# Expert weights of a mixture-of-experts stage loaded as two 1 MB transfers for each 2 MB slot

## The reference

```python
logits = (xt @ w_router + b_router).astype(jnp.float32)
top_vals, top_idx = lax.top_k(logits, TOP_K)          # 4 of 32 experts for each token
gates = jax.nn.softmax(top_vals, axis=-1)
...
def expert_block(args):
    xb, e = args
    hgu = xb @ w_up_gate[e] + b_up_gate[e]            # [1024, 2048]: 8 MB
    x_glu = jnp.minimum(hgu[:, :D_EXPERT], SWIGLU_LIMIT)
    x_lin = jnp.clip(hgu[:, D_EXPERT:], -SWIGLU_LIMIT, SWIGLU_LIMIT)
    hact = x_glu * jax.nn.sigmoid(SWIGLU_ALPHA * x_glu) * (x_lin + 1.0)
    return hact @ w_down[e] + b_down[e]               # [1024, 1024]: 4 MB
```

## Time and profile before

| | |
|---|---|
| Time, median of 3 runs | 1893.27 us (1886.38, 1893.27, 1894.21) |
| The profiled execution | 1885.67 us, its span 1883.9 us, mean granted TensorE clock 0.988 |
| TensorE matmuls busy | 1760.2 us, 93% of the span |
| VectorE, ScalarE, GpSimd busy | 774.7, 499.6, 209.3 us |
| DMA | 554.26 MB, 294 GB/s over the span, queue q1 72.6% |

### The profile page before, as it was taken

One profiled execution on the slowest core, in us unless ns is written; L12 is line 12 of the kernel. 1 busy time (PEld: TensorE's weight loads), 2 busy tenths in 40 slices (PEclk: granted clock), 3 DMA queues, 4 the chain that ended last, 5 costly groups with the idle time before them and its releaser, 6 DMA issues. The chain is left out here.

```text
span 1883.9 us, 28671 instructions
## 1 busy us (share of the span) xinstructions
PE 1760.2 (93%) x11617; PEld 1096.0 (58%) x11617; DVE 774.7 (41%) x1312; ACT 499.6 (27%) x784; POOL 209.3 (11%) x150
## 2 busy tenths in 40 slices
PE   8999999999999898988889889999999999999997
PEld 7774333333333333333333368978998768858996
DVE  7956111111111111111011186947555767346555
ACT  5644000000000000000000056436443331225552
POOL 5552000000000000000000045430000100410000
PEclk9999999999999999999999999999999989899999
DMA  7289999999999999999999946475530622256530
GB/s 285 101 310 403 383 426 428 430 430 429 430 429 430 431 429 430 429 430 430 430 429 429 398 142 260 159 266 204 197 134 21 209 92 53 105 179 225 193 118 34
DMA packets 104729, 554.26 MB, mean 294 GB/s; under 512 B 17442, under 2 KB 27683, under 8 KB 79219
## 3 DMA queue, kind: packets, MB, share of 16 engines
q1 hardware_dynamic: 104370, 553.25, 72.6%
q10 hardware_dynamic: 288, 0.02, 0.0%
HBM read 551.15 MB, written 2.10 MB: 294 GB/s over the span
## 5 line engine op out<-in xcount | busy, mean ns | idle before, releaser
L1365 PE MATMUL banks<-front,xsT 128*64 128x512 f32 x1344 | 298.4, 594 | 14.1 <-DMA front<-in_w_up 13.6
L1581 DVE TENSOR_SCALAR xT<-banks 128x512 f32<-128x512 f32 x32 | 22.1, 692 | 625.4 <-PE banks L1372 625.4
L1365 PEld LDWEIGHTS banks<-front,xsT 128*64 128x64 f32 x1344 | 95.7, 137 | 209.6 <-issue 178.4
L1405 PE MATMUL banks<-front,hT 128*64 128x512 f32 x704 | 159.3, 606 | 15.9 <-ACT hT L1480 15.9
L2356 PE MATMUL banks<-f_xT_hi,f_w_hi 128*128 128x256 f32 x512 | 144.9, 283 | 3.0 <-DVE f_xT_lo L319 3.0
L1476 ACT ACTIVATE xT<-xT 128x512 f32<-128x512 f32 x32 | 20.1, 629 | 475.4 <-DVE xT L1581 475.3
L2356 PE MATMUL banks<-f_xT_hi,f_w_lo 128*128 128x256 f32 x512 | 144.9, 283 | 0.0
L2356 PE MATMUL banks<-f_xT_lo,f_w_hi 128*128 128x256 f32 x512 | 144.9, 283 | 0.0
L1405 PEld LDWEIGHTS banks<-front,hT 128*64 128x64 f32 x704 | 50.2, 139 | 109.8 <-issue 99.3
L1710 POOL TENSOR_TENSOR p_w_lo<-p_w_raw,p_w_hi 128x1024 fp32r<-128x1024 f32 x4 | 11.6, 2929 | 910.0 <-ACT p_w_hi L1752 910.0
L2445 DVE TENSOR_TENSOR f_w_lo<-f_ring,f_w_hi 128x1024 fp32r<-128x1024 f32 x64 | 77.9, 1225 | 63.1 <-ACT f_w_hi L2398 63.1
(11 more groups left out here) (474 smaller groups left out, 3071.0 us busy)
## 6 DMA issues: line engine op xcount, KB each, us to landing
front<-in_w_up SPq DMA_DIRECT2D x84, 2048.0 KB, 32.9
front<-in_w_down SPq DMA_DIRECT2D x44, 2048.0 KB, 34.3
f_ring<-in_ffn_w SPq DMA_DIRECT2D x30, 2048.0 KB, 7.6
m_early_slots<-in_w_up SPq DMA_DIRECT2D x22, 2048.0 KB, 27.9
more_slots<-in_w_up SPq DMA_DIRECT2D x22, 2048.0 KB, 33.0
m_early_slots<-in_w_down SPq DMA_DIRECT2D x20, 2048.0 KB, 37.1
g_ring<-in_sgu_in SPq DMA_DIRECT2D x7, 2048.0 KB, 7.6
m_raw<-in_w_in SPq DMA_DIRECT2D x6, 2048.0 KB, 8.2
```

The source lines that it names most:

```text
L1365: ins = nc.tensor.matmul(c.banks[CAP * h:CAP * (h + 1), bank, :], xsT[:, k, :], up[:, o:o + BANK], start=k == 0, stop=False)
L1405: ins = nc.tensor.matmul(c.banks[CAP * h:CAP * (h + 1), DOWN, :], hT[:, at:at + CAP], down[:, o:o + BANK], start=k == 0, stop=k == KC - 1)
L1581: v.tensor_scalar(glu[:, :], c.banks[:, GLU, :], LIMIT, None, ALU.min).then_inc(glu_ready, 1)
```

## The change

Each load of a slot becomes two transfers, of columns 0 to 2047 and 2048 to 4095 of the slot, 1 MB each, and each half has a landing semaphore of its own. TensorE waits for a half before the first chunk that reads it (one chunk of up, two chunks of down) and counts `up_used` and `down_used` by halves, twice as many for an item. SyncE waits for the half of the old load that lies where the half of the new one goes. All thresholds are doubled to match. The order of the loads, the slots, the matmuls and the bytes are the same. The early loads of the mixer stage go in halves too, behind the same waits as before. `product` is that of itertools. The core of the diff:

```diff
+HALVES, HALF_SLOT = 2, SLOT // 2
-        self.up_in = [sem(f"up_in{q}") for q in range(UPS)]
+        self.up_in = [[sem(f"up_in{q}_{half}") for half in range(HALVES)] for q in range(UPS)]
...
-    def load_up(self, sp, e, q, slot=None, landed=None):
-        sp.dma_start(slot or self.slot(UP_SLOT[q]), self.dram["w_up"][bass.ds(e * P, P), q * SLOT:(q + 1) * SLOT]).then_inc(
-            landed or self.up_in[q], 16)
+    def load_up(self, sp, e, q, slot=None, landed=None, halves=range(HALVES)):
+        slot = slot if slot is not None else self.slot(UP_SLOT[q])
+        for half in halves:
+            at = half * HALF_SLOT
+            sp.dma_start(slot[:, at:at + HALF_SLOT],
+                         self.dram["w_up"][bass.ds(e * P, P), q * SLOT + at:q * SLOT + at + HALF_SLOT]).then_inc(
+                (landed or self.up_in[q])[half], 16)
...
                 def item(n, one):
-                    for s in range(FRONT):
+                    for s, half in product(range(FRONT), range(HALVES)):
...
-                                sp.wait_ge(up_used, n * (3 * UPS) + ((one + ago) * UPS + last + 1))
+                                sp.wait_ge(up_used, n * (3 * UPS * HALVES) + (
+                                    ((one + ago) * UPS + last) * HALVES + half + 1))
...
-                            load(n * 3 + one, s, lap_and_slot(flat)[1])
+                            load(n * 3 + one, s, lap_and_slot(flat)[1], (half,))
...
-                def weights(i, n):
+                def weights(i, n, half):
...
-                        pe.wait_ge(landed[at], i[0] * 32 + 16 * (lap + 1))
+                        pe.wait_ge(landed[at][half], i[0] * 32 + 16 * (lap + 1))
...
-                        if k % 2 == 0:
-                            up = weights(i, k // 2)
+                        up = weights(i, k // 2, k % 2)
...
-                        if k % 2 and k < KC - 1:
+                        if k < KC - 1:
                             ins.then_inc(up_used, 1)
...
-                        if j == 0:
-                            down = weights(i, UPS + half)
+                        if j % 2 == 0:
+                            down = weights(i, UPS + half, j // 2)
...
-                        if j == KC // 2 - 1:
+                        if j % 2:
                             ins.then_inc(down_used, 1)
...
-                    act.wait_ge(down_used, i * DOWNS + DOWNS)
+                    act.wait_ge(down_used, i * (DOWNS * HALVES) + DOWNS * HALVES)
...
-                    dve.wait_ge(up_used, i * UPS + UPS)
+                    dve.wait_ge(up_used, i * (UPS * HALVES) + UPS * HALVES)
```

More of the change, by code:

```diff
@@ L1 @@
 from contextlib import ExitStack
+from itertools import product
 import numpy as np
@@ L142, in open_experts @@
             "router_in", "r_const_in", "list_in", "b_down_in"))
-        self.up_in = [sem(f"up_in{q}") for q in range(UPS)]
-        self.down_in = [sem(f"down_in{h}") for h in range(DOWNS)]
-        self.early_in = [sem(f"early_in{q}") for q in range(EARLY)]
+        self.up_in = [[sem(f"up_in{q}_{half}") for half in range(HALVES)] for q in range(UPS)]
+        self.down_in = [[sem(f"down_in{h}_{half}") for half in range(HALVES)] for h in range(DOWNS)]
+        self.early_in = [[sem(f"early_in{q}_{half}") for half in range(HALVES)] for q in range(EARLY)]
     def slot(self, i):
@@ L151, in early_slot, with load_down @@
         return self.early_slots[:, i * SLOT:(i + 1) * SLOT]
-    def load_up(self, sp, e, q, slot=None, landed=None):
-        sp.dma_start(slot or self.slot(UP_SLOT[q]), self.dram["w_up"][bass.ds(e * P, P), q * SLOT:(q + 1) * SLOT]).then_inc(
-            landed or self.up_in[q], 16)
-    def load_down(self, sp, e, h, slot=None, landed=None):
-        sp.dma_start(slot or self.slot(DOWN_SLOT[h]), self.dram["w_down"][bass.ds(e * (2 * P) + h * P, P), :]).then_inc(
-            landed or self.down_in[h], 16)
+    def load_up(self, sp, e, q, slot=None, landed=None, halves=range(HALVES)):
[5 more added lines that the diff above has]
+                (landed or self.up_in[q])[half], 16)
+    def load_down(self, sp, e, h, slot=None, landed=None, halves=range(HALVES)):
+        slot = slot if slot is not None else self.slot(DOWN_SLOT[h])
+        for half in halves:
+            at = half * HALF_SLOT
+            sp.dma_start(slot[:, at:at + HALF_SLOT],
+                         self.dram["w_down"][bass.ds(e * (2 * P) + h * P, P), at:at + HALF_SLOT]).then_inc(
+                (landed or self.down_in[h])[half], 16)
     def load_expert_tables(self, sp):
@@ L1103, in expert_stage @@
         slots += [more[:, i * SLOT:(i + 1) * SLOT] for i in (1, 0)]
-        landed = c.up_in + c.down_in + c.early_in + [sem(f"slot_in{i}") for i in range(FRONT + EARLY, SPARE + 1)]
+        landed = c.up_in + c.down_in + c.early_in + [
+            [sem(f"slot_in{i}_{half}") for half in range(HALVES)] for i in range(FRONT + EARLY, SPARE + 1)]
         squares = slots[RING - 1][:, 0:TC * D].rearrange("p (c n) -> p c n", c=TC)
@@ L1191, in _, with load @@
             def _(sp):
-                def load(e, n, at):
+                def load(e, n, at, halves=range(HALVES)):
                     if n < UPS:
-                        c.load_up(sp, e, n, slots[at], landed[at])
+                        c.load_up(sp, e, n, slots[at], landed[at], halves)
                     else:
-                        c.load_down(sp, e, n - UPS, slots[at], landed[at])
+                        c.load_down(sp, e, n - UPS, slots[at], landed[at], halves)
                 def item(n, one):
-                    for s in range(FRONT):
+                    for s, half in product(range(FRONT), range(HALVES)):
                         flat = FRONT * one + s
@@ L1204, in item @@
                             if last < UPS:
-                                sp.wait_ge(up_used, n * (3 * UPS) + ((one + ago) * UPS + last + 1))
-                            else:
-                                sp.wait_ge(down_used, n * (3 * DOWNS) + ((one + ago) * DOWNS + last + 1 - UPS))
+                                sp.wait_ge(up_used, n * (3 * UPS * HALVES) + (
+                                    ((one + ago) * UPS + last) * HALVES + half + 1))
+                            else:
+                                sp.wait_ge(down_used, n * (3 * DOWNS * HALVES) + (
+                                    ((one + ago) * DOWNS + last - UPS) * HALVES + half + 1))
                         if flat == RING:
-                            load(one, s, SPARE)
-                            sp.wait_ge(root_done, 1)
-                            load(one, s - 1, RING - 1)
+                            load(one, s, SPARE, (half,))
+                            if half == HALVES - 1:
+                                sp.wait_ge(root_done, 1)
+                                load(one, s - 1, RING - 1)
                         elif flat >= FRONT + EARLY and flat != RING - 1:
-                            load(n * 3 + one, s, lap_and_slot(flat)[1])
+                            load(n * 3 + one, s, lap_and_slot(flat)[1], (half,))
                 def late_item(i, e):
-                    for s in range(FRONT):
+                    for s, half in product(range(FRONT), range(HALVES)):
                         if s < UPS:
-                            sp.wait_ge(up_used, i * UPS + (s + 1 - UPS))
+                            sp.wait_ge(up_used, i * (UPS * HALVES) + ((s - UPS) * HALVES + half + 1))
                         else:
-                            sp.wait_ge(down_used, i * DOWNS + (s - UPS + 1 - DOWNS))
-                        load(e, s, lap_and_slot(FRONT * (E - 1) + s)[1])
+                            sp.wait_ge(down_used, i * (DOWNS * HALVES) + ((s - UPS - DOWNS) * HALVES + half + 1))
+                        load(e, s, lap_and_slot(FRONT * (E - 1) + s)[1], (half,))
                 sp.dma_start(chooser[:, :], c.dram["chooser"]).then_inc(chooser_in, 16)
@@ L1233, in _ @@
                     late_item(i, listed_at(sp, i + EXPERT_AT, E - 1))
-                sp.wait_ge(down_used, DOWNS * (E - 1))
+                sp.wait_ge(down_used, DOWNS * HALVES * (E - 1))
                 c.next_embedding.load(sp)
@@ L1344, in weights @@
                     if isinstance(i, tuple):
-                        pe.wait_ge(landed[at], i[0] * 32 + 16 * (lap + 1))
+                        pe.wait_ge(landed[at][half], i[0] * 32 + 16 * (lap + 1))
                     elif isinstance(i, int):
-                        pe.wait_ge(landed[at], 16 * (lap + 1))
+                        pe.wait_ge(landed[at][half], 16 * (lap + 1))
                     else:
-                        pe.wait_ge(landed[at], i * 16 + 16 * (lap + 1 - (E - 1)))
+                        pe.wait_ge(landed[at][half], i * 16 + 16 * (lap + 1 - (E - 1)))
                     return slots[at]
```

## The result

| | Before | Changed |
|---|---|---|
| Median of 22 runs each | 1886.29 us (1878.84 to 1894.21) | 1894.54 us (1887.08 to 1902.51) |
| Ratio to before | | 1.0036, 95% interval 1.0020 to 1.0052 |
| The profiled execution, its span | 1885.67, 1883.9 us | 1900.08, 1898.3 us |

The changed kernel is slower by 0.36%, 6.8 us of 1886.29 (3.8 to 9.8); the two medians are 8.25 us apart, which lies in that interval. The interval is clear of 1, the size is within the 0.5% that the prediction called no change, and the forecast was 15.4 us. Two of the three runs that the prediction had for a base lay at the upper end of what 22 runs show, and so did their median, 1893.27. Of the 14.2 us between the forecast 1908.7 and the median measured, 7.0 are the base, and the other 7.2 are the size of the change.

The account below looks back on a forecast made before the run. DMA, busy without a gap through the expert stage, was taken as the bound. 19.0 us for shorter rows less 1.8 at the gap and 1.8 at the tail gave +15.4 on the median 1893.27: 1908.7 us, range 1894 to 1919.

Parts of the forecast that it names:

- The bound: Expert stage: DMA busy without a gap at 429.5 GB/s, 29.30 us an expert; TensorE needs 27.2 and late on follows DMA.
- The gap: DMA runs dry near 218 us, waiting for expert 1's first down slot; reloading by halves restarts it earlier, gain 1.8 us.
- The tail: Last expert: TensorE starts on the first half of the last up slot while the second lands, gain 1.8 us.
- The edits at nothing: TensorE's added waits, SyncE's added issues, doubled thresholds and the embedding weights behind the expert loads: claimed to cost nothing.
- The time of a slot: Expert loads: rows of 8 KB instead of 16 KB cost 0.110 us a slot, 19.0 us over 173 loads.
- the division of the rows into queued transfers and lone ones: Price of an added packet: 11.8 to 13.8 ns where transfers queue, 5.6 to 5.7 ns alone; expert loads counted as queued.
- the 435 GB/s rival: Expert stage: twice the transfers keep the queue fuller and DMA at 435 GB/s; -14.3 us, 1879 us; chance 0.10.
- The lone-transfer price: Expert loads: packets cost as in a lone transfer, 45 ns a slot; +4.2 us, 1897.5 us; chance 0.24.
- More transfers in flight: Expert stage: a deeper queue makes loads faster, 4.821 us a slot, 0.76% faster in all; chance 0.10.
- the bytes alone did not set the rate: Expert loads: rival that 8 KB packets move as fast as 16 KB ones, leaving two gains; -3.6 us, 1889.7; chance 0.06.
- TensorE did not become the bound: Expert stage: rival that each new wait breaks TensorE's pipeline for 0.5 us, 30.2 us an expert; 1919 us; chance 0.02.

## Why the prediction was right and wrong

*The bound* was right: from 232 us to the end of the expert loads DMA had no gap in the changed kernel, nor in any other run but the one with the short queue, and late in the stage TensorE follows it. The late pace is 29.55 us an expert (952.02 to 981.57 in the changed kernel; forecast 29.9), 29.23 before.

*The gap* was right for the issue, 1.72 us sooner for 1.77, and wrong for what that is worth. The sum let the whole 1.8 us reach the end since no new gap opens; none does, but DMA moves slower behind the issue, and some 0.9 us reach the end. *The tail* was right: 1.71 for 1.75, and the profile showed it, though the down matmuls behind it took as much longer at a lower clock in that execution.

*The edits at nothing* were right. The issues of SyncE did become slower and DMA stayed full; the added waits of TensorE left the early pace at 27.22 us (509.46 to 536.68).

*The time of a slot* is the term that failed, in size. The mechanism was right: cut rows at unchanged bytes, paid for by the packet. The price was 0.063 us a slot (2,097,152 bytes at 424 GB/s are 4.946 us), 10.9 us for 173 loads, where the sum had 0.110 and 19.0. With 10.9 in place of 19.0 the sum is +7.3 us, and with 0.9 for the gap +8.2; measured were 6.8 (3.8 to 9.8). That the median, 1894.54 us, still lies at the lower edge of the forecast's range, 1894 to 1919, is luck: the base was 7.0 us lower, and the size is under the 12.7 us with which the working of that range begins. What failed in the term are two choices. The first is the division of the rows into queued transfers and lone ones, by which the dear rows were taken for the expert loads: the runs show 7.6 to 7.9 ns, and the same rate with a queue half as deep. The second is to trust a window of 4 us to the third figure. A window that short has an edge error of a packet on each engine, 16 x 8 KB in 1.68 MB, 8% at most; the same row shape was worth 420 GB/s there and is 424 in a stretch of 462 us. Moved by 1 us either way, that window of the kernel before reads 428 or 410:

```profile
1132.00:1136.00 4.00, 4.00 (x19) 3.31 (x18) 3.72 (x12) 0.00 (x0) 1.23 (x1) 1.00 1.05 428
...
1134.00:1138.00 4.00, 4.00 (x19) 3.34 (x18) 3.62 (x16) 0.36 (x1) 0.00 (x0) 1.00 1.00 410
```

The argument against the 435 GB/s rival was just this, and it was not turned on the forecast's own row.

*The rivals.* The lone-transfer price (+4.2 us, within 0.5%) had 0.24 and came nearer than the forecast; it lies within the interval, 3.8 to 9.8, and its 5.6 ns are still too few for the 424 GB/s. More transfers in flight were not faster, the bytes alone did not set the rate, and TensorE did not become the bound. The Trainium skill's page DMA: Bandwidth & Descriptors (Why small descriptors are slow) gives about 3 cycles for a packet, by which the estimate was 3.5 ns; the trace agrees in sign and has 7.6 to 7.9.

## What to carry to other kernels

Where a stream of loads has no gap, only three things of it reach the end: its first moment, its rate and what is left behind its last landing. Finer transfers help the first and the last once, some 0.9 and 1.7 us here, and a shorter row is paid in every load. So if loads are cut at all, cut only those at the two ends; the run that did so was 1.7 us ahead in its time line, which its times could not tell from nothing. Keep rows whole: splitting a slot by partitions cost 1.3 us over 171 loads, splitting its rows 10.5. Read the price of a packet from stretches of hundreds of microseconds, or make such a stretch, before it is multiplied by 173.

## What the runs showed of the hardware

Rows of 16, 8 and 4 KB, back to back onto 128 partitions, move at 429 to 430, 424 and 414 GB/s: each added packet of an engine makes a slot 7.6 to 7.9 ns longer, and the 8 KB rows move at 424 GB/s as one transfer of 2 MB or as two of 1 MB. With 1 MB transfers that land 26.8 us after their issue SyncE's issues take 1.85 us, with ones that land after 14.2 us 0.33, and the stream does not feel it. The spread of the runs goes with the clock: the 22 runs of the changed kernel go from 1887.08 us at a mean granted clock of 0.990 to 1902.51 at 0.985, and the seven that are under 1890 us all have 0.989 or more, the five above 1899 us 0.985 or less.
